# Latent attention: weighted values of two heads, block by block in turn, at the end of each pair of heads

## The chip, the cores and the metric

One NeuronCore of a Trainium2 chip runs the kernel. The metric is the device time of one execution in microseconds. PE is the matrix engine (TensorE), PEld its weight loads, DVE VectorE, ACT ScalarE, POOL GpSimd, SP the engine that issues most DMAs.

## The reference, cut to what matters

One layer of a decoder: half a feed-forward step, a mixer of two attention branches, another half feed-forward step, for 512 tokens of width 1024. The part that the change touches is the latent attention of the mixer, with 8 heads, query and key of 96 numbers, values of 64, causal over 512 tokens:

```python
def causal_dense_attention(q, k, v, scale):
    ...
    def one_block(args):
        qb, qp = args
        logits = jnp.einsum('bqhd,bkhd->bhqk', qb, k).astype(jnp.float32) * scale
        logits = jnp.where(k_pos[None, :] <= qp[:, None], logits, NEG_INF)
        p = jax.nn.softmax(logits, axis=-1)
        return jnp.einsum('bhqk,bkhd->bqhd', p.astype(v.dtype), v)
```

The last line is the product of probabilities and values. Its result goes on, with that of a dilated attention of 24 heads, through two projections, gates and an output projection.

## The kernel before, in words

All activations lie transposed, features on the partitions and the 512 tokens along the free axis. The program is one stream of weight pieces of 128 x 1024 numbers. Each is loaded by a DMA into `raw`, rounded by ScalarE into `w_hi` (`split_hi`, line 352), its rest taken by VectorE into `w_lo` (`split_lo`, line 357), and used by TensorE in three products per 128 x 128 tile (`multiply`, lines 370 to 372). The order of each engine's work is written out by hand, and engines wait for one another by semaphores; each engine runs its own list in order.

The latent stage does one head per turn, two heads per round of the loop (line 644), then heads 6 and 7 outside it. In head h TensorE does, in `attention` (line 616):

- `score` (line 567): the scores of head h into banks 2, 3 and 4, four blocks of 128 queries against all keys up to them, each with one product that adds the causal mask;
- `turn_values` (line 558): values of head h turned into bank 5, from where ScalarE copies them to `mla_v` (`take_values`, line 941);
- `lora` (line 548): key, value and query of head h + 1, 15 products; VectorE takes them in `take_lora` (lines 1295 to 1313), key and values (`mla_k`, `mla_vt`) first;
- `project` (line 517): 24 products of a gate, and ahead of the last two tiles of it, in `turn_early`, the probabilities of head h turned for the first key block (part 0) and the second (part 1). Head 7 has the first dilated projection in place of the gate, and no `lora`;
- `turn_probs(h, i, 2)`: the third and fourth key blocks turned (part 2);
- `attend` (line 599), once for each part: products of values and turned probabilities into bank 7. Key block k reaches queries from k on, so the four products are 512, 384, 256 and 128 columns wide. An even head fills partitions 0 to 63 of the bank, an odd one 64 to 127.

Parts go through banks 6, 5 and 6 and are copied by ScalarE (`take_probs`, line 953) to one of two buffers of `probs_t` in turn, so the third copy has to wait until the first part has been used (`pv_done`, line 960). Behind the three copies ScalarE has the gate's tanh (line 936) and the split of the next weights (line 352). VectorE has, per head, `maxima` (line 1316) on the scores, `take_lora` with `normalize` (line 1325) inside it, the splits of weights, and after an odd head `take_mixed` (line 1334), the copy of the pair's results out of bank 7. The lines that the rows below name are 961 (copies of turned probabilities), 610 (products with values), 595 (transposes), 579 and 581 (scores, mask), 1320 (maxima), 1308 (the next query is ready), 1313 (`mla_vt`).

The dilated stage behind it handles two heads at once, and its `attend_dil` (line 694) alternates between the two, head e in partitions 64 e to 64 e + 63 of bank 2 (lines 703 and 707).

Of the kernel before, what the change touches and what calls it, by code (L numbers as in the profile page):

```python
# [32 lines left out]
P = 128  # L33
SEQ = 512
BLOCKS = SEQ // P
# [11 lines left out]
PAIRS = GROUP_HEADS // 2  # L47
# [148 lines left out]
def decoder_layer(nc, x_t, positions, rel_bias, gains_in, tables, onehot_in, mask_in, ffn, w_latent, w_lora_up,  # L196
# [22 lines left out]
    with ctx:  # L219
# [44 lines left out]

        mixed = shared("mixed", [P, 2 * PAIRS, SEQ])
        gates = shared("gates", [P, 2 * KM, SEQ])
        probs_t = shared("probs_t", [P, 2, SEQ])
        lat_hi = shared("lat_hi", [P, KQ + KKV, SEQ], F32R)
        lat_lo = shared("lat_lo", [P, KQ + KKV, SEQ], F32R)
        sumsq_kv = shared("sumsq_kv", [P, SEQ])  # L270
# [4 lines left out]
        mla_q = shared("mla_q", [P, 2, SEQ])  # L275
        mla_k = shared("mla_k", [P, 2, SEQ])
        mla_vt = shared("mla_vt", [P, SEQ])
        mla_v = shared("mla_v", [P, BLOCKS, V_DIM])
        mla_p = shared("mla_p", [P, 10 * P])
        mask_ident = shared("mask_ident", [P, P], F32R)  # L280
        mask_causal = shared("mask_causal", [P, P], F32R)
# [182 lines left out]
        def _(pe):  # L464
# [102 lines left out]
            def score(h, i):  # L567

                pe.wait_ge(head_ready, h + 2 * i + 1)
                for b, (out, diagonal) in enumerate(((bank[2][:, 0:P], bank[2][:, 0:P]),
                                                     (bank[3][:, 0:2 * P], bank[3][:, P:2 * P]),
                                                     (bank[2][:, P:SEQ], bank[2][:, 3 * P:SEQ]),
                                                     (bank[4][:, :], bank[4][:, 3 * P:SEQ]))):
                    nc.tensor.matmul(out, mla_q[0:QK_DIM, h % 2, b * P:(b + 1) * P],  # L579
                                     mla_k[0:QK_DIM, h % 2, 0:(b + 1) * P], start=True, stop=False, skip_group_check=True)  # L580
                    last = nc.tensor.matmul(diagonal, mask_ident[:, :], mask_causal[:, :], start=False, stop=True,
                                            skip_group_check=True)
                last.then_inc(mla_scores, 1)
# [12 lines left out]
                        at += P  # L596
                last.then_inc(turned, 1)

            def attend(h, i, part):

                unit = 4 * h + 1 + part
                pe.wait_ge(turned_taken, unit + 8 * i + 1)
                row = V_DIM * (h % 2)
                at = 0
                for key in ((0,), (1,), (2, 3))[part]:
                    width = SEQ - key * P
                    last = nc.tensor.matmul(bank[7][row:row + V_DIM, key * P:SEQ], mla_v[:, key, :],  # L610
                                            probs_t[:, (3 * h + part) % 2, at:at + width],
                                            start=key == 0, stop=key == 3, skip_group_check=True)
                    at += width
                last.then_inc(pv_done, 1)

            def attention(h, i, s, d):

                score(h, i)
                turn_values(h, i)

                def turn_early(k):
                    if k == 6:
                        turn_probs(h, i, 0)
                        turn_probs(h, i, 1)

                if h < MLA_HEADS - 1:
                    lora(s, d, h + 1, i)
                    c = gate_chunk(h)
                    project(s + 1, d, c + 6 * i, bank[c % 2][:, :], turn_early)
                else:  # L630

                    c = CHUNKS["dil"]
                    project(PIECES["dil"], 0, c, bank[c % 2][:, :], turn_early)
                turn_probs(h, i, 2)
                for part in range(3):
                    attend(h, i, part)

            s = PIECES["mla"]

# [170 lines left out]
        def _(act):  # L810
# [127 lines left out]

            def take_values(h, i):
                act.wait_ge(turned, 4 * h + 8 * i + 1)  # L940
                nc.scalar.copy(mla_v[:, :, :].rearrange("p b n -> p (b n)"),
                               bank[5 + (4 * h) % 2][:, 0:BLOCKS * V_DIM]).then_inc(turned_taken, 1)

            def exponentials(h, i):
# [6 lines left out]
                                         accum_out=mla_stats[:, 2, b:b + 1]).then_inc(mla_exp, 1)  # L951

            def take_probs(h, i):
                for part, width in enumerate((4 * P, 3 * P, 3 * P)):
                    unit = 4 * h + 1 + part
                    act.wait_ge(turned, unit + 8 * i + 1)
                    n = 3 * h + part
                    if n >= 2:

                        act.wait_ge(pv_done, n + 6 * i - 1)  # L960
                    nc.scalar.copy(probs_t[:, n % 2, 0:width], bank[5 + unit % 2][:, 0:width]).then_inc(turned_taken, 1)

            def attention(h, i, s, d, following):

# [35 lines left out]
            def take_dil_probs(unit, i):  # L1000
                width = 3 * P if unit // 2 == 1 else SEQ
                act.wait_ge(turned, 4 * MLA_HEADS + unit + 8 * i + 1)

                act.wait_ge(pv_done, 3 * MLA_HEADS + unit + 8 * i - 1)
                nc.scalar.copy(probs_t[:, unit % 2, 0:width], bank[5 + unit % 2][:, 0:width]).then_inc(turned_taken, 1)

            def dilated_pair(i, first=False):
# [53 lines left out]
        def _(dve):  # L1061
# [288 lines left out]
            def attention(h, i, s, d, following):  # L1350


                maxima(h, i)
                if h < MLA_HEADS - 1:
                    take_lora(s, d, h + 1, i, lambda: normalize(h, i))
                    split_lo(dve, s + 2, d, following[0])
                    gate_take(s + d + 2, gate_chunk(h) % 2, h + 1 + 2 * i)
                    if following[1]:
                        split_lo(dve, s + 3, d, following[1])
                else:  # L1360
                    normalize(h, i)
                    split_lo(dve, s + 2, d, following[0])
                if h % 2:
                    take_mixed(h // 2 + i, 3 * h + 3 + 6 * i, bank[7][:, :])

            s = PIECES["mla"]
            take_lora(s, 0, 0, 0, query_norm_and_rotary_key)
# [105 lines left out]
            def dilated_pair(i, first=False):  # L1473
                s, d, c, e = PIECES["dil"], 12 * i, CHUNKS["dil"], 11 * i
                for q in range(12):
                    tiles = HALF if q in (9, 10) else TILES
                    if q or not first:
                        split_lo(dve, s + q + 1, d, tiles)
                    if q in (3, 5, 7):
                        dil_maxima(q // 2 - 1, i)  # L1480
                    if q < 6:
                        out = (dil_q, dil_k)[q % 2][:, q // 2, :]
                    else:
                        out = dil_vt[:, q % 2, :]
                    if q == 0 and not first:

                        take_mixed(PAIRS - 1 + i, 3 * MLA_HEADS + 8 * i, bank[2][:, :])
                    if q < 9:
                        take_projection(out, s + q, d, (c + q) % 2)
                    if q == 9:  # L1490
                        group_weights(i)
                        scale_probs(0)
                        gate_take(s + d + 10, (c + 9) % 2, MLA_HEADS + 2 * i)
                        for g in (1, 2):
                            scale_probs(g)
# [6 lines left out]

            for k in range(2 * PAIRS):
                if k == PAIRS:
                    take_mixed(2 * PAIRS - 1, 3 * MLA_HEADS + 8 * PAIRS, bank[2][:, :])
                dve.wait_ge(mixed_rounded, k + 1)
                nc.vector.tensor_tensor(act_lo[:, k, :], mixed[:, k, :], act_hi[:, k, :].bitcast(F32),
                                        ALU.subtract).then_inc(mixed_split, 1)
# [113 lines left out]
```

## Time and profile before

| | us |
|---|---|
| median of 3 runs | 1325.17 (1324.86 to 1326.73) |
| the profiled execution | 1325.78 |
| its span, first to last instruction | 1323.2 |
| TensorE busy | 1296.1 (98%) |
| VectorE busy | 673.4 (51%) |
| ScalarE busy | 437.9 (33%) |
| latent stage, heads 0 to 7, in the span | about 424 to 550 |

A matmul record in the profile has a start and a modelled end, and records of one engine overlap, so the distance from start to start tells what a product costs. An f32 product has two records and two weight loads. A line of the timeline that ends in x8 is eight records that lie together, from the first start to the last end.

### The profile page before, as it was taken

To read this page: it belongs to the slowest core of one execution; us is meant where nothing else is said; L and a number is where in the kernel's file an instruction comes from. 1 tells how busy PE (TensorE), PEld (TensorE's weight loads), DVE (VectorE), ACT (ScalarE), POOL (GpSimd) and SP (SyncE) were. 2 spreads that over 40 slices of the span, in tenths; PEclk is the share of its full clock that TensorE was granted. 3 is DMA by queue.
4 is the path that set the end of the run, shared out by engine and by line. 5 is a ranking of instruction groups with operands and counts; after the bars stand their busy time and mean duration, and the time that the engine had idled before them with its cause. 6 is when DMAs were issued, how large, how long until landed. Compare 5 with 4: busy or idle time off the path is not lost.

```text
span 1323.2 us, 16875 instructions
## 1 busy us (share of the span) xinstructions
PE 1296.1 (98%) x5984; PEld 1042.1 (79%) x5984; DVE 673.4 (51%) x947; ACT 437.9 (33%) x763; POOL 16.4 (1%) x34
## 2 busy tenths in 40 slices
PE   8999999999998999999999999999999999999996
PEld 5788888888886677788887878778888888888884
DVE  6744444433358666454554445476654444443324
ACT  5322223322243344243433333433432222332221
POOL 0000000000000000300000000000000000000000
PEclk9999999999999999999999999999999999999998
DMA  6243332233322211612222122223323322223321
GB/s 222 80 111 98 100 100 96 88 103 90 102 89 62 68 52 64 127 64 80 72 72 80 63 79 69 74 80 98 109 80 97 99 101 98 96 89 91 98 87 63
DMA packets 35920, 118.84 MB, mean 90 GB/s; under 512 B 4664, under 2 KB 4664, under 8 KB 35888
## 3 DMA queue, kind: packets, MB, share of 16 engines
q1 hardware_dynamic: 34272, 114.83, 27.1%
q0 software_dynamic: 1328, 3.56, 1.6%
q8 instruction: 19, 0.31, 0.1%
q14 instruction: 13, 0.11, 0.0%
q10 hardware_dynamic: 288, 0.03, 0.0%
HBM read 115.85 MB, written 2.55 MB: 89 GB/s over the span
## 4 chain that ended last, share of the span: by engine, by line
PE 90%; DVE 6%; ACT 2%; issue 1%; DMA 1%; SPq 0%; DVEq 0%; ACTq 0%
PE bank L370 27%; PE bank L372 27%; PE bank L371 27%; PE bank L667 2%; PE bank L610 1%; PE bank L579 1%; PE bank L690 1%; DVE w_lo L357 1%; ACT w_hi L352 1%; DVE rstd L1098 1%; DMA raw<-in_ffn_up 1%; PE bank L595 1%; PE bank L707 1%; PE bank L703 1%; PE bank L676 0%
## 5 line engine op out<-in xcount | busy, mean ns | idle before, releaser
L370 PE MATMUL bank<-act_hi,w_hi 128*128 128x512 f32 x1232 | 487.8, 396 | 7.7 <-DVE w_lo L357 3.6
L372 PE MATMUL bank<-act_hi,w_lo 128*128 128x512 f32 x1232 | 480.1, 390 | 0.0
L371 PE MATMUL bank<-act_lo,w_hi 128*128 128x512 f32 x1232 | 479.8, 389 | 0.0
L357 DVE TENSOR_TENSOR w_lo<-raw,w_hi 128x1024 fp32r<-128x1024 f32 (+3 forms) x222 | 260.3, 1172 | 240.3 <-ACT w_hi L352 236.1
L352 ACT ACTIVATE w_hi<-raw 128x1024 fp32r<-128x1024 f32 (+3 forms) x222 | 224.0, 1009 | 200.1 <-PE bank L372 199.7
L370 PEld LDWEIGHTS bank<-act_hi,w_hi 128*128 128x128 f32 x1232 | 231.3, 188 | 65.3 <-issue 8.9
L372 PEld LDWEIGHTS bank<-act_hi,w_lo 128*128 128x128 f32 x1232 | 231.3, 188 | 49.1
L371 PEld LDWEIGHTS bank<-act_lo,w_hi 128*128 128x128 f32 x1232 | 231.5, 188 | 46.7 <-issue 1.0
L372 PE MATMUL bank<-hid_hi,w_lo 128*128 128x512 f32 x352 | 136.9, 389 | 0.0
L370 PE MATMUL bank<-hid_hi,w_hi 128*128 128x512 f32 x352 | 136.9, 389 | 0.0
L371 PE MATMUL bank<-hid_lo,w_hi 128*128 128x512 f32 x352 | 136.9, 389 | 0.0
L859 ACT ACTIVATE hid_hi<-work 128x512 f32 (+1 forms) x44 | 27.8, 633 | 171.9 <-DVE work L1170 171.9
L857 ACT ACTIVATE work<-work 128x512 f32<-128x512 f32 x44 | 27.8, 632 | 154.9 <-DVE work L1164 154.9
L371 PEld LDWEIGHTS bank<-hid_lo,w_hi 128*128 128x128 f32 x352 | 66.1, 188 | 13.8
L370 PEld LDWEIGHTS bank<-hid_hi,w_hi 128*128 128x128 f32 x352 | 66.1, 188 | 13.7
L372 PEld LDWEIGHTS bank<-hid_hi,w_lo 128*128 128x128 f32 x352 | 66.1, 188 | 13.5
L1164 DVE TENSOR_TENSOR work<-bank,rstd 128x512 f32<-128x512 f32 x44 | 30.4, 691 | 63.0 <-PE bank L372 62.9
L1170 DVE TENSOR_TENSOR work<-bank,work 128x512 f32<-128x512 f32 x44 | 30.4, 692 | 56.0 <-PE bank L372 55.6
L1175 DVE TENSOR_TENSOR hid_lo<-work,hid_hi 128x512 f32 (+1 forms) x44 | 30.5, 693 | 43.1 <-ACT hid_hi L859 43.1
L993 ACT ACTIVATE dil_p<-dil_p,stats 128x128 f32<-128x128 f32 (+1 forms) x96 | 39.9, 416 | 37.0 <-DVE stats L1411 37.0
L817 ACT ACTIVATE act_hi<-x,gains 128x512 fp32r<-128x512 f32 (+1 forms) x24 | 16.9, 721 | 67.5 <-DVE x L1193 38.0
L1193 DVE SCALAR_TENSOR_TENSOR x<-bank,x 128x512 f32 (+1 forms) x16 | 11.1, 692 | 44.6 <-PE bank L372 44.6
(153 smaller groups left out, 929.2 us busy)
## 6 DMA issues: line engine op xcount, KB each, us to landing
raw<-in_ffn_gate SPq DMA_DIRECT2D x44, 512.0 KB, 3.4
raw<-in_ffn_up SPq DMA_DIRECT2D x44, 512.0 KB, 3.4
raw<-in_w_dil SPq DMA_DIRECT2D x40, 512.0 KB, 3.4
raw<-in_ffn_down SPq DMA_DIRECT2D x32, 448.0 KB, 3.3
raw<-in_ffn_down SPq DMA_DIRECT2D x16, 512.0 KB, 3.5
raw<-in_w_mla_gates SPq DMA_DIRECT2D x8, 512.0 KB, 3.4
raw<-in_w_branches SPq DMA_DIRECT2D x8, 512.0 KB, 3.4
raw<-in_w_out SPq DMA_DIRECT2D x8, 512.0 KB, 3.4
```

What stands on the lines that cost most here:

```text
L352: nc.scalar.activation(w_hi[:, s % SPLIT, 0:tiles * P], raw[:, s % RAW, 0:tiles * P], ACT.Copy).then_inc(hi_ready, 1)
L357: nc.vector.tensor_tensor(w_lo[:, s % SPLIT, 0:tiles * P], raw[:, s % RAW, 0:tiles * P], w_hi[:, s % SPLIT, 0:tiles * P].bitcast(F32), ALU ...
L370: nc.tensor.matmul(out, a, hi(k), start=first, stop=False)
L371: nc.tensor.matmul(out, a, lo(k), start=False, stop=False)
L372: last = nc.tensor.matmul(out, b, hi(k), start=False, stop=end)
L667: last = nc.tensor.matmul(out, dil_q[rows, g, tokens(g, b)], dil_k[rows, g, keys], start=True, stop=True, skip_group_check=True)
L857: nc.scalar.activation(work[:, 1, :], work[:, 0, :], ACT.Silu).then_inc(silu_ready, 1)
L859: nc.scalar.activation(hid_hi[:, bass.ds(2 * i + j, 1), :], work[:, 3:4, :], ACT.Copy).then_inc(hid_rounded, 1)
L993: nc.scalar.activation(p, p, ACT.Exp, bias=stats[:, 0, g, order, at:at + 1], accum_out=stats[:, 1, g, order, at:at + 1]).then_inc(dil_exp, 1)
L1164: nc.vector.tensor_tensor(work[:, 0, :], bank[c % UP_BANKS][:, :], rstd[:, :], ALU.mult).then_inc(chunk_taken, 1)
L1170: nc.vector.tensor_tensor(work[:, 3, :], bank[c % UP_BANKS][:, :], work[:, 2, :], ALU.mult).then_inc(chunk_taken, 1)
L1175: nc.vector.tensor_tensor(hid_lo[:, chunk, :], work[:, 3:4, :], hid_hi[:, chunk, :].bitcast(F32), ALU.subtract).then_inc(hid_split, 1)
```

## The change

The tile `probs_t` becomes 2 x 1280 numbers per partition instead of 2 x 512: all ten turned blocks of one head in each half, odd heads in one, even in the other. `mla_v` has two buffers, one per head of a pair. ScalarE's copies no longer wait for `pv_done`. `attend` runs after odd heads alone and does both heads: for each key block the product of the even head, then that of the odd head. `pv_done` goes up once per pair and no longer once per part, and the waits on it are counted anew (the copies of the dilated stage, `take_mixed`). Ahead of an odd head's scores TensorE waits for the even head's first two copies, a wait that `attend` of the even head had made before.

```diff
-        probs_t = shared("probs_t", [P, 2, SEQ])
+        probs_t = shared("probs_t", [P, 2, 10 * P])
...
-        mla_v = shared("mla_v", [P, BLOCKS, V_DIM])
+        mla_v = shared("mla_v", [P, 2, BLOCKS, V_DIM])
...
+                if h % 2:
+                    pe.wait_ge(turned_taken, 4 * h + 8 * i - 1)
                 pe.wait_ge(head_ready, h + 2 * i + 1)
...
-            def attend(h, i, part):
-
-
-
-
-                unit = 4 * h + 1 + part
-                pe.wait_ge(turned_taken, unit + 8 * i + 1)
-                row = V_DIM * (h % 2)
-                at = 0
-                for key in ((0,), (1,), (2, 3))[part]:
+            def attend(h, i):
+
+                for key in range(BLOCKS):
+                    part, at = ((0, 0), (1, 4 * P), (2, 7 * P), (2, 9 * P))[key]
+                    pe.wait_ge(turned_taken, 4 * h + 2 + part + 8 * i)
                     width = SEQ - key * P
-                    last = nc.tensor.matmul(bank[7][row:row + V_DIM, key * P:SEQ], mla_v[:, key, :],
-                                            probs_t[:, (3 * h + part) % 2, at:at + width],
-                                            start=key == 0, stop=key == 3, skip_group_check=True)
-                    at += width
+                    for e in range(2):
+                        last = nc.tensor.matmul(bank[7][V_DIM * e:V_DIM * (e + 1), key * P:SEQ], mla_v[:, e, key, :],
+                                                probs_t[:, e, at:at + width], start=key == 0, stop=key == BLOCKS - 1,
+                                                skip_group_check=True)
                 last.then_inc(pv_done, 1)
...
                 turn_probs(h, i, 2)
-                for part in range(3):
-                    attend(h, i, part)
+                if h % 2:
+                    attend(h, i)
...
-                nc.scalar.copy(mla_v[:, :, :].rearrange("p b n -> p (b n)"),
+                nc.scalar.copy(mla_v[:, h % 2, :, :].rearrange("p b n -> p (b n)"),
...
-                for part, width in enumerate((4 * P, 3 * P, 3 * P)):
+                for part, (at, width) in enumerate(((0, 4 * P), (4 * P, 3 * P), (7 * P, 3 * P))):
                     unit = 4 * h + 1 + part
                     act.wait_ge(turned, unit + 8 * i + 1)
-                    n = 3 * h + part
-                    if n >= 2:
-
-                        act.wait_ge(pv_done, n + 6 * i - 1)
-                    nc.scalar.copy(probs_t[:, n % 2, 0:width], bank[5 + unit % 2][:, 0:width]).then_inc(turned_taken, 1)
+                    nc.scalar.copy(probs_t[:, h % 2, at:at + width], bank[5 + unit % 2][:, 0:width]).then_inc(turned_taken, 1)
...
-                    take_mixed(h // 2 + i, 3 * h + 3 + 6 * i, bank[7][:, :])
+                    take_mixed(h // 2 + i, h // 2 + i + 1, bank[7][:, :])
```

The end of an even head on TensorE, before (`const,mla_p` are the transposes of probabilities, `probs_t,mla_v` the products with values, `mla_k,mla_q` the next head's scores):

```order
L595 MATMUL bank<-const,mla_p 128x128 [waits turned_taken]
L595 MATMUL bank<-const,mla_p 128x128 x2
L610 MATMUL bank<-probs_t,mla_v 64x512 [waits turned_taken]
L605 REGISTER_ALU
L610 MATMUL bank<-probs_t,mla_v 64x384 [waits turned_taken]
L610 MATMUL bank<-probs_t,mla_v 64x256 [waits turned_taken]
L610 MATMUL bank<-probs_t,mla_v 64x128
L574 REGISTER_ALU
L579 MATMUL bank<-mla_k,mla_q 128x128 [waits head_ready]
L581 MATMUL bank<-mask_causal,mask_ident 128x128
```

The same place in the changed program:

```order
L597 MATMUL bank<-const,mla_p 128x128 [waits turned_taken]
L597 MATMUL bank<-const,mla_p 128x128 x2
L575 REGISTER_ALU
L576 REGISTER_ALU [waits turned_taken]
L581 MATMUL bank<-mla_k,mla_q 128x128 [waits head_ready]
L583 MATMUL bank<-mask_causal,mask_ident 128x128
```

The four products are gone from here, and the scores follow the transposes.

The end of an odd head on TensorE, in the changed program:

```order
L597 MATMUL bank<-const,mla_p 128x128 [waits turned_taken]
L597 MATMUL bank<-const,mla_p 128x128 x2
L608 MATMUL bank<-probs_t,mla_v 64x512 [waits turned_taken]
L608 MATMUL bank<-probs_t,mla_v 64x512
L605 REGISTER_ALU
L608 MATMUL bank<-probs_t,mla_v 64x384 [waits turned_taken]
L608 MATMUL bank<-probs_t,mla_v 64x384
L608 MATMUL bank<-probs_t,mla_v 64x256 [waits turned_taken]
L608 MATMUL bank<-probs_t,mla_v 64x256
L608 MATMUL bank<-probs_t,mla_v 64x128 [waits turned_taken]
L608 MATMUL bank<-probs_t,mla_v 64x128
```

Each width stands twice, even head first, and the waits are for ScalarE's copies of the odd head.

## Rows read from the trace of the kernel before

**Rows 1.** The page: busy time of each engine, and the chain that ended last.

```profile
PE 1296.1 (98%) x5984; PEld 1042.1 (79%) x5984; DVE 673.4 (51%) x947; ACT 437.9 (33%) x763; POOL 16.4 (1%) x34
...
PE 90%; DVE 6%; ACT 2%; issue 1%; DMA 1%; SPq 0%; DVEq 0%; ACTq 0%
```

**Rows 2.** Busy time by stretches: stretch, length, PE, PEld, DVE, ACT, POOL, PE clock, DMA.

```profile
430.00:560.00 130.00, 128.13 (x590) 92.81 (x589) 80.44 (x150) 49.44 (x118) 12.71 (x24) 1.00 0.29 75
```

**Rows 3.** The same view, line 610 alone: PE and PEld busy, clock, DMA.

```profile
439.62:442.06 2.44, 2.44 (x8) 0.93 (x8) 1.00 0.47 134
...
547.82:550.31 2.49, 2.49 (x8) 0.93 (x8) 1.00 0.49 194
sum 19.59, PE 19.58 PEld 7.42; mean PE 2.45 PEld 0.93
```

**Rows 4.** Timeline of TensorE, end of head 0: start, duration, work.

```profile
439.20 0.49 PE L595 MATMUL bank<-const,mla_p 128*128 128x128 f32 x3
439.62 2.50 PE L610 MATMUL bank<-probs_t,mla_v 128*64 128x512 f32 x8
442.06 0.49 PE L579 MATMUL bank<-mla_k,mla_q 96*128 96x128 f32 x2
```

**Rows 5.** The same, windows 439.65 to 440.05, then to 440.20.

```profile
439.42 0.27 PE L595 MATMUL bank<-const,mla_p 128*128 128x128 f32 x1
439.62 0.64 PE L610 MATMUL bank<-probs_t,mla_v 128*64 128x512 f32 x1
...
439.62 1.07 PE L610 MATMUL bank<-probs_t,mla_v 128*64 128x512 f32 x2
```

**Rows 6.** The same, dilated stage, windows to 612.10, to 612.30, to 612.95.

```profile
611.90 0.44 PE L703 MATMUL bank<-probs_t,dil_v 128*64 128x256 f32 x2
...
611.90 0.65 PE L703 MATMUL bank<-probs_t,dil_v 128*64 128x256 f32 x4
...
611.90 1.08 PE L703 MATMUL bank<-probs_t,dil_v 128*64 128x256 f32 x8
612.91 0.33 PE L690 MATMUL bank<-const,dil_p 128*128 128x128 f32 x1
```

**Rows 7.** Busy time by stretches, instructions on `dil_v` alone: PE, clock, DMA.

```profile
618.66:619.68 1.02, 1.02 (x16) 1.00 0.00 0
```

**Rows 8.** Waits of the weight loader, heads 0 to 7: total us, times, longest.

```profile
PEld bank L610 <- ACT probs_t L961: 4.8, 8, 0.6
```

**Rows 9.** Timeline of ScalarE, head 0 (in brackets: idle before, and what ended it).

```profile
437.69 0.97 ACT L961 COPY probs_t<-bank 128x512 f32<-128x512 f32 x2 [3.49 <-PE bank L595]
440.73 0.48 ACT L961 COPY probs_t<-bank 128x384 f32<-128x384 f32 x1 [2.07 <-PE bank L610]
...
441.73 1.05 ACT L352 ACTIVATE w_hi<-raw 128x1024 fp32r<-128x1024 f32 x1
```

**Rows 10.** Timeline of VectorE, end of head 0 and start of head 1.

```profile
437.25 0.68 DVE L1308 TENSOR_TENSOR mla_q<-mla_q,rotated 32x512 f32<-32x512 f32 x1
...
442.81 1.23 DVE L357 TENSOR_TENSOR w_lo<-raw,w_hi 128x1024 fp32r<-128x1024 f32 x1 [2.72 <-ACT w_hi L352]
444.92 1.69 DVE L1320 TENSOR_REDUCE mla_stats<-bank 128x1 f32<-128x128 f32 x4 [0.89 <-PE bank L581]
```

**Rows 11.** Timelines of VectorE and TensorE: head 0's maxima, then both gate projections.

```profile
429.51 1.68 DVE L1320 TENSOR_REDUCE mla_stats<-bank 128x1 f32<-128x128 f32 x4
...
432.01 0.69 DVE L1313 TENSOR_TENSOR mla_vt<-bank,rstd_kv 64x512 f32<-64x512 f32 x1
...
432.84 0.49 PE L370 MATMUL bank<-act_hi,w_hi 128*128 128x512 f32 x1 [0.87 <-DVE mla_vt L1313]
...
448.73 0.39 PE L370 MATMUL bank<-act_hi,w_hi 128*128 128x512 f32 x1
```

**Rows 12.** Weight loads: line 610's (ns min/median/max), then the timeline in the dilated stage.

```profile
L610 PEld LDWEIGHTS bank<-probs_t,mla_v x64: 132/136/137, 439.6 to 550.0; 128*64 128x64 f32 x64
...
611.89 0.63 PEld L703 LDWEIGHTS bank<-probs_t,dil_v 128*64 128x64 f32 x8 [0.36 <-ACT probs_t L1005]
```

More of the change, by code:

```diff
@@ L1002, in take_dil_probs @@
                 act.wait_ge(turned, 4 * MLA_HEADS + unit + 8 * i + 1)
-                act.wait_ge(pv_done, 3 * MLA_HEADS + unit + 8 * i - 1)
+                act.wait_ge(pv_done, PAIRS + unit + 8 * i - 1)
                 nc.scalar.copy(probs_t[:, unit % 2, 0:width], bank[5 + unit % 2][:, 0:width]).then_inc(turned_taken, 1)
@@ L1485, in dilated_pair @@
                     if q == 0 and not first:
-                        take_mixed(PAIRS - 1 + i, 3 * MLA_HEADS + 8 * i, bank[2][:, :])
+                        take_mixed(PAIRS - 1 + i, PAIRS + 8 * i, bank[2][:, :])
                     if q < 9:
@@ L1504, in _ @@
                 if k == PAIRS:
-                    take_mixed(2 * PAIRS - 1, 3 * MLA_HEADS + 8 * PAIRS, bank[2][:, :])
+                    take_mixed(2 * PAIRS - 1, PAIRS + 8 * PAIRS, bank[2][:, :])
                 dve.wait_ge(mixed_rounded, k + 1)
```

## Prediction

> **What bounds the kernel now.** I read the page first: TensorE is busy for 98% of the span, VectorE for 51%, ScalarE for 33%, and the chain that ended last is 90% TensorE work [rows 1]. So a microsecond taken out of TensorE's queue is a microsecond of the whole, as long as the other engines keep up. The table by stretches says that this holds where the change is, in the latent stage, and that the clock granted there is full: 128.13 of 130 us busy at 1.00 [rows 2]. At full clock (the 2.4 GHz level) nothing is to be won or lost from the clock, and I take none.
>
> Then I cut out the weighted values alone. Each head spends 2.44 us on them from the first record of `bank<-probs_t,mla_v` to the first record of what follows, the last two heads 2.49; eight stretches make 19.59 us, 1.5% of the span [rows 3]. In head 0 they lie between the last transposes and the next head's scores with nothing of another kind in between [rows 4]. That is the whole of what the change can speed up directly.
>
> How do those 2.44 us arise? Each of the four products of a head is an f32 product and leaves two records. A window of TensorE's timeline that ends at 440.05 holds one 512-column record, one that ends at 440.20 holds two, and together they last 1.07 against 0.64 us: the second starts 0.43 us behind the first [rows 5]. So the records of one head run in turn, 512 columns per 0.43 us. For 512 + 384 + 256 + 128 = 1,280 columns in two records each this makes 2 x 1,280 x 0.43 / 512 = 2.15 us, and 0.29 us are left for the way in, the way out and a stall. Each such product fills 64 of the array's 128 columns (128*64 in the rows).
>
> The trace already has the pattern that the change brings, in the dilated stage: there the two heads of a pair alternate product by product, one head's result in partitions 0 to 63 of the bank, the other's in 64 to 127. Two 256-column records start together at 611.90 and take 0.44 us in all, four take 0.65 (in turn the second alone would end there), and from the first of eight to the start of the next kind of work at 612.91 it is 1.01 us [rows 6]. In turn the eight would take 8 x 0.43 / 2 = 1.72 us. In pairs they take 4 x 0.215 = 0.86, and 0.15 is left for way in and out. The sixteen 128-column records say the same: 1.02 us [rows 7] against 16 x 0.107 = 1.72 in turn and 0.86 in pairs.
>
> **The change, part by part.**
>
> *Even heads (0, 2, 4, 6)* lose their whole stretch: TensorE goes from the third group of transposes straight to the next head's scores. That removes 3 x 2.44 + 2.49 = 9.81 us.
>
> *Odd heads* now do both heads, 16 records, alternating. If they pair up as in the dilated stage, the time is 2 x (0.43 + 0.32 + 0.215 + 0.107) = 2.14 us, plus the 0.15 of way in and out from [rows 6]: 2.29 us, where 2.44 or 2.49 stood. Four stretches of 2.29 are 9.2 us; against 19.6 that is **10.4 us less**.
>
> *The stall inside a head.* Before, the third copy of turned probabilities waited until the first product had freed its buffer, and the weight loads of the third product waited for that copy: 4.8 us in all over eight heads, 0.6 at most [rows 8]. Most of it is not lost on TensorE, since a product was still running; what is lost is part of the 0.29 us above. With both heads' probabilities kept, the copy doesn't wait for a product, and it overlaps the first four products of the pair (1.5 us against a copy of 0.48). It is already counted: the 2.29 has no stall. Nothing is late next there.
>
> *The new wait ahead of an odd head's scores* (the first two copies of the even head must be done). In head 0 these copies end at 437.69 + 0.97 = 438.66 [rows 9], and the scores would want to start at 439.62, where the products stood [rows 4]. It costs nothing, with 0.96 us to spare. Behind it stand the scores and all else of the next head, so a late ScalarE would be felt at once. The scores also want the query of the next head, which VectorE has ready at 437.25 + 0.68 = 437.93 [rows 10]: 1.7 us to spare.
>
> *ScalarE after an even head.* The third copy now starts when its transposes are done (439.20 + 0.49 [rows 4], about 439.8) and not at 440.73. The gate's tanh and the split of the next weights are queued behind it and move with it, by 0.95 us; in the rows of before the split starts at 441.73 [rows 9], so it starts near 440.8 and VectorE's half of the split, which stood at 442.81 [rows 10], near 441.9.
>
> *VectorE after an even head.* Here the cover is thin. The scores now end 2.44 us sooner, so the maxima could start at 444.92 - 2.44 = 442.48, but the split of weights stands ahead of them on VectorE and ends at 441.9 + 1.23 = 443.1. The maxima are 0.6 us late against TensorE. From their start to the end of `mla_vt` it takes 432.01 + 0.69 - 429.51 = 3.19 us when nothing is waited for, so `mla_vt` is done at 446.3, and TensorE starts 0.14 us behind it (432.70 and 432.84 in head 0, where the same lateness costs 0.87 us once [rows 11]). The gate projection would want to start at 448.73 - 2.44 = 446.29 [rows 11]. So it stands for about 0.1 us in each of heads 0, 2 and 4; after head 6 no such products follow. I put **0.3 us** on this. Bounds: nothing, if ScalarE's part moves up by 0.1 more; and if nothing of ScalarE's moved up, the split would end at 444.04 and the stall would be 1.0 us, 3 us over three heads.
>
> *Odd heads, other engines.* ScalarE's third copy and what is behind it move up by the same 0.95 us while TensorE's products shrink by 0.15 only. The copy of the finished pair out of the bank stands between the split and the maxima as before, and has more room. Buffers: the larger tiles cost memory and no instruction. The loads of weights are released by the split, and TensorE waits for none of them here.
>
> *Switches of the array's mode.* Between the last transpose and the first product, and again before the scores, the weight loader pauses; of eight such pairs four go. The stretches of [rows 3] run from start to start, so this is inside the 2.44 already.
>
> The sum: 10.4 - 0.3 = 10.1 us less. The profiled execution took 1325.78 us (span 1323.2 and 2.6 around it), so 1315.7 for it; the median of the runs shown is 0.6 lower, and my number is **1315.1 us**.
>
> **A rule against it.** The rows show eight loads of 64 columns done within 0.63 us while the paired products of the dilated stage run [rows 12]; a load alone takes 0.137. The Trainium skill ("TensorE: Matmul & The Clock Gate", Part 3, on packing small matmuls) says that a weight load overlaps running products only when its row group differs. Here both heads use all 128 rows and differ in columns only. By that rule the 16 loads of a pair would stand bare.
>
> **The rivals.**
>
> *Loads or products don't overlap between the two heads.* With 16 bare loads of 0.137 us, the pair takes 2.29 + 2.19 = 4.5 us; with products in turn 2 x 2.36 - 0.15 = 4.57. Either way 0.3 to 0.4 us per pair is won against 4.88, in all about 1.5 us: **1323.6 us**, no change to be told. [Rows 6, 12] speak against it. For it speaks only that the trace of before has no 512-column products that alternate. Chance 0.04.
>
> *Only half pairing.* If a head's second record has to wait behind its first while the other head's has not begun, the 16 records take one 512-column step more: 2.29 + 0.43 = 2.72 us per pair, and the gain is 8.4 us: 1316.8. Chance 0.12.
>
> *VectorE becomes the bound after even heads.* With 1.0 us of stall in three heads, as bounded above, the gain is 7.4 us: 1317.8. The row of 0.87 us in [rows 11] shows that the mechanism is real; the copy that moves up speaks against its full size. Chance 0.13.
>
> *Slower: alternating costs a switch each time.* The Trainium skill ("TensorEngine Tiling (Array Packing)", Key Properties) says that a change of tiling mode drains the engine, and that a change of tile alone doesn't. If on this chip the step from one half of the columns to the other did, there would be 15 such steps in 16 records or 7 between the products. By rows: products in turn, 4.57 us, and 7 steps of 0.20 us, the largest distance that the transposes show ahead of a change (439.42 to 439.62 [rows 4, 5]), make 5.97 against 4.88, 4.4 us more in all: **1329.6 us**. It is slower from 0.05 us a step. The two records that start together in [rows 6] exclude it, unless 512 columns differ from 256. Chance 0.02.
>
> **How the numbers follow.** Forecast 0.69, half pairing 0.12, VectorE 0.13, no overlap 0.04, switches 0.02. A measurement of this kernel tells about 0.2%, 2.6 us, from no change. The first three are all faster by more than that, so faster 0.94; no change 0.04; slower 0.02. The likely case alone spans 1314.3 (no stall, and a better way out of even heads by 0.1 each) to 1316.4. The range reaches to the half pairing and to VectorE's bound with some room for the chip: 1313.4 to 1318.2.
>
> **What would show it.** In the profile after: the products in four stretches of about 2.3 us, each with 16 records, two 512-column records starting together; no product between an even head's transposes and the next scores; a full clock. For the small term: TensorE idle before the gate projection put down to `mla_vt`, 0.1 us in three heads. Stretches of 4.5 us would make me wrong on the pairing, idle of about 1 us behind even heads wrong on VectorE, and a gain in the latent stage that the span doesn't show would mean that the dilated stage waits for something else than TensorE.

## The result, and the profile after

The changed kernel takes 1318.97 us (median of 4 executions, 1318.42 to 1319.48), the kernel before, run beside it, 1325.93 (4 executions, 1324.86 to 1326.73). The medians lie 7.0 us apart, a ratio of 0.9948; the ratio on record, which is not taken from these two medians alone, is 0.9941, 95% interval 0.9928 to 0.9953 (6.2 to 9.5 us). Either way the kernel is faster, clear of the noise. The profiled execution took 1319.48 us against 1325.78, its span 1317.5 against 1323.2.

The forecast was 1315.1 us, a gain of 10.1, with a range of 1313.4 to 1318.2: the direction is right, the time lies 0.8 us above the range, and 3 of the 10 us are missing. The kernel before was 0.8 us slower in this comparison than the 1325.17 that the forecast starts from; as a gain the range was 7.0 to 11.8 us, and the measured gain lies at its lower edge. Where the missing 3 us are is the subject of this part. The page first, busy time and the chain that ended last, against [rows 1]:

```profile
PE 1291.8 (98%) x5984; PEld 1043.4 (79%) x5984; DVE 672.7 (51%) x947; ACT 438.5 (33%) x763; POOL 16.4 (1%) x34
...
PE 89%; DVE 6%; ACT 2%; issue 1%; DMA 1%; DVEq 0%; SPq 0%; ACTq 0%
```

Nothing has changed sides: TensorE is 98% busy. The products with values, in the busy time by stretches (PE, PEld, clock, DMA), against [rows 3]:

```profile
457.23:459.53 2.30, 2.30 (x16) 1.05 (x16) 1.00 0.53 142
486.46:488.75 2.29, 2.29 (x16) 1.06 (x16) 1.00 0.54 143
515.69:517.98 2.29, 2.29 (x16) 1.06 (x16) 1.00 0.78 222
542.26:544.56 2.30, 2.30 (x16) 1.06 (x16) 1.00 0.58 217
sum 9.18, PE 9.18 PEld 4.23; mean PE 2.29 PEld 1.06
```

Four stretches of 16 records in 9.18 us stand where eight of 8 records took 19.59. The timeline of TensorE shows the pair, in windows that end at 457.60 and at 457.80, against [rows 5]:

```profile
457.23 0.65 PE L608 MATMUL bank<-probs_t,mla_v 128*64 128x512 f32 x2
...
457.23 1.08 PE L608 MATMUL bank<-probs_t,mla_v 128*64 128x512 f32 x4
```

Two 512-column records last 0.65 us where one lasted 0.64, and four last 1.08 where two lasted 1.07. The two heads run at the same time. At the end of head 0 the scores follow the transposes directly, against [rows 4]:

```profile
443.21 0.49 PE L597 MATMUL bank<-const,mla_p 128*128 128x128 f32 x3
443.54 0.28 PE L581 MATMUL bank<-mla_k,mla_q 96*128 96x128 f32 x1
```

So 10.4 us of products are gone, and the span is only 5.7 shorter. Two things took most of the rest. The first is in the busy time by stretches of TensorE alone (PE busy, clock, DMA), before the first changed instruction has run:

```profile
422.00:425.00 3.00, 1.26 (x6) 1.00 0.00 0
425.00:426.00 1.00, 0.49 (x3) 0.83 0.00 0
426.00:435.00 9.00, 9.00 (x24) 0.50 0.31 96
435.00:436.00 1.00, 1.00 (x4) 0.55 0.00 0
436.00:445.00 9.00, 9.00 (x48) 1.00 0.14 38
```

TensorE had stood still ahead of head 0's scores (2.25 us by the wait on the row below), and then its clock was at the lower of its two levels, 1.2 GHz, for some 10 us: 24 records in nine of them. The same stretches of the kernel before:

```profile
422.00:425.00 3.00, 0.86 (x4) 1.00 0.00 0
425.00:426.00 1.00, 0.90 (x6) 1.00 0.00 0
426.00:435.00 9.00, 8.13 (x36) 1.00 0.30 96
```

There the idle time is the same and the clock stayed full. The first score after the wait, in the changed kernel, then in the kernel before:

```profile
425.51 0.68 PE L581 MATMUL bank<-mla_k,mla_q 96*128 96x128 f32 x2 [2.25 <-DVE mla_q L1301]
```

```profile
425.10 0.49 PE L579 MATMUL bank<-mla_k,mla_q 96*128 96x128 f32 x2 [2.24 <-DVE mla_q L1308]
```

From these scores to the first transposes of head 0 it takes 15.6 us (425.51 to 441.07) in the changed kernel and 11.9 (425.10 to 437.05) before. That is 3.6 us for the lower clock, and it hides the 0.87 us of [rows 11], which is idle time no longer. The scores themselves start 0.4 us later than before (425.51 against 425.10), ahead of any instruction that differs, so 0.4 us of the two spans' difference is the start of the execution.

The second thing is what the prediction had as a small term. In the timeline of the changed kernel, last product of `lora` and first of the gate behind it, after head 0:

```profile
449.89 0.39 PE L372 MATMUL bank<-lat_hi,w_lo 128*128 128x512 f32 x1
450.45 0.49 PE L370 MATMUL bank<-act_hi,w_hi 128*128 128x512 f32 x1 [0.17 <-DVE mla_vt L1306]
```

From start to start 0.56 us, where without a wait it is 0.23 (448.51 to 448.73 before). The same place after heads 2 and 4 has 0.52 and 0.51. So TensorE loses 0.33 + 0.29 + 0.28 = 0.9 us. And the product behind such a wait holds up the next one by 0.1:

```profile
450.78 0.39 PE L371 MATMUL bank<-act_lo,w_hi 128*128 128x512 f32 x1
```

which is 0.33 us behind its forerunner and not 0.23. Together the three waits cost 1.2 us, where 0.3 was forecast. The column "idle" shows only 0.17 of the first, since it counts from the modelled end of the last product: the distance of starts is what tells.

### The profile page after: what moved, and what is told of

It reads as the page before. It is cut to its first block, busy times and chain, and to the rows that moved or that the text cites. A ratio compares the mean times of both kernels' runs of the same rounds, so it can differ in the third digit from the quotient of the medians.

```text
span 1317.5 us, 16858 instructions
## 1 busy us (share of the span) xinstructions
PE 1291.8 (98%) x5984; PEld 1043.4 (79%) x5984; DVE 672.7 (51%) x947; ACT 438.5 (33%) x763; POOL 16.4 (1%) x34
## 4 chain that ended last, share of the span: by engine, by line
PE 89%; DVE 6%; ACT 2%; issue 1%; DMA 1%; DVEq 0%; SPq 0%; ACTq 0%
PE bank L370 28%; PE bank L372 27%; PE bank L371 27%; PE bank L664 2%; PE bank L581 1%; PE bank L687 1%; DVE w_lo L357 1%; ACT w_hi L352 1%; DVE rstd L1091 1%; PE bank L608 1%; DMA x<-in_x_t 1%; PE bank L597 1%; PE bank L704 1%; PE bank L700 1%; DVE mla_stats L1313 1%
```

## The experiments

**First the clock.** Both kernels again, unchanged, in more executions, and both with the idle time ahead of head 0's scores filled. The filled kernels have, at the end of TensorE's work ahead of the loop, products of constants into a bank that is free there; nobody reads their results:

```diff
             project(s + 1, 0, gate_chunk(-1), bank[gate_chunk(-1) % 2][:, :])
+            for width in (SEQ, SEQ, 2 * P):
+                nc.tensor.matmul(bank[6][:, 0:width], ident, const[:, C_EXPAND:C_EXPAND + width], start=True, stop=True)
```

The kernel before, again:

> The kernel before, unchanged, to see in several executions whether the clock granted to TensorE stays full through the idle time ahead of head 0's scores. Theory A (the lower clock of the changed kernel from 425.8 to 435.5 us is a matter of where the idle time of 2.9 us happens to fall, not of the new order, which begins later): some executions here show a mean clock near 0.992 and are about 3 us longer than the others. Theory B (the change causes it): all executions show 0.997 and lie within 1 us of 1325.5.

Measured: 12 executions from 1324.39 to 1329.98, median 1327.76, mean clocks from 0.991 to 0.997. The times go with the clock: three at 0.997 (1324.39 to 1325.64), three at 0.994 (1326.65 to 1326.80), six at 0.991 and 0.992 (1328.73 to 1329.98).

The changed kernel, again:

> The changed kernel, unchanged, again in several executions. Theory A: some executions show a mean clock of 0.997 and about 1316 us, the others 0.992 and 1319. Theory B: all show 0.992 and 1319.

Measured: two executions at 0.997 (1314.97 and 1315.04), two at 0.994 (1316.79, 1316.80), two at 0.992 (1319.11, 1319.23). Theory A holds in both kernels: the lower clock comes in the kernel before just as well, in 9 of these 12 executions. At like clocks the changed kernel is faster by 9.9 to 10.3 us: 1325.25, the middle of the three at 0.997, against 1315.0; 1326.7 against 1316.8; 1329.3, the median of the six, against 1319.2. In the first comparison all four executions of the changed kernel had 0.992 or 0.993, while the one clock that is recorded for the kernel before is 0.997; by their times two of its four executions (1324.86, 1325.17) belong to the full clock and two (1326.69, 1326.73) to the middle group. The middle group has a shorter stretch at the lower level; the profile of such an execution of the changed kernel shows it (TensorE alone, as above):

```profile
422.00:426.00 4.00, 1.76 (x10) 1.00 0.00 0
426.00:427.00 1.00, 1.00 (x4) 0.61 0.65 118
427.00:433.00 6.00, 6.00 (x17) 0.50 0.37 124
433.00:434.00 1.00, 1.00 (x6) 0.98 0.00 0
```

Of the kernel before no execution with a lower clock was profiled: that its slow stretch lies in the same place is argued from its mean clocks and from the next run.

The kernel before with the idle time filled:

> The kernel before with three products of constants into a free bank (512, 512 and 256 columns, 2.1 us) in TensorE's idle time ahead of head 0's scores. Both theories: the clock stays full there. It should measure as the kernel before does at full clock, 1325.2, or up to 0.3 us more if the last of them delays the scores.

Measured: 1324.94 (11 executions, 1324.14 to 1325.22), clocks 0.995 to 0.997. Adding work makes this kernel faster than the unfilled one beside it (ratio 0.9981, interval 0.9971 to 0.9991), and its times lie within 1.1 us and not 5.6.

The changed kernel, filled:

> The changed kernel with the same three products. If the lower clock is what hid the rest of the gain, the clock is full and the time is about 1316.0 (9.4 us below the filled kernel before: 10.5 of products less 1.0 of stalls behind VectorE). If something else keeps the gain down to 7 us, it stays near 1319.

Measured: **1314.74** (5 executions, 1314.34 to 1315.04), all at 0.996 or 0.997, ratio to the unfilled kernel before 0.9909 (0.9895 to 0.9922). Against the filled kernel before it is 10.2 us faster. TensorE in its timeline, the filling products and the scores behind them:

```profile
422.13 2.31 PE L642 MATMUL bank<-const 128*128 128x512 f32 x6
424.52 0.49 PE L581 MATMUL bank<-mla_k,mla_q 96*128 96x128 f32 x2
```

and no 2.2 us of idle time. The scores start 0.6 us earlier than those of the filled kernel before (425.15), and nothing differs between the two programs up to there, so 0.6 of the 10.4 us between the two profiled spans is the start of the execution and not the change.

**Then the gain, part by part**, all with the filling products. The runs of this part and of the next come from a second chip, the last two runs from a third. The fastest executions of the unfilled kernel before were 1324.42, 1324.38 and 1324.91 us on the three, so a few tenths between medians of different chips tell nothing, and lengths within one profile are given beside them.

The two heads in series at the end of a pair:

```diff
-                for key in range(BLOCKS):
-                    part, at = ((0, 0), (1, 4 * P), (2, 7 * P), (2, 9 * P))[key]
-                    pe.wait_ge(turned_taken, 4 * h + 2 + part + 8 * i)
-                    width = SEQ - key * P
-                    for e in range(2):
+                for e in range(2):
+                    for key in range(BLOCKS):
+                        part, at = ((0, 0), (1, 4 * P), (2, 7 * P), (2, 9 * P))[key]
+                        pe.wait_ge(turned_taken, 4 * (h - 1 + e) + 2 + part + 8 * i)
+                        width = SEQ - key * P
```

> The changed kernel with the three filling products, but at the end of a pair the four products of the even head come first and then the four of the odd head; nothing else differs. Theory A (the gain comes from products of the two heads that run at the same time in different columns): the stretch goes from 2.30 to about 4.57 us per pair, and the time is 9.1 us above the filled changed kernel, near 1323.8. Theory B (the gain comes from the waits and the fewer changes between kinds of work, and alternating adds little): the stretch stays near 2.3 to 3, and the time within 2 us of 1314.7.

Measured: 1321.10 (1320.64 to 1321.59), 6.4 us above the alternating one. Theory A is right in kind and 2.7 us off in size. The stretch is 3.86 us and not 4.57, as the timeline of TensorE and the chain of the same stretch show:

```profile
452.89 3.93 PE L608 MATMUL bank<-probs_t,mla_v 128*64 128x512 f32 x16
456.75 0.49 PE L581 MATMUL bank<-mla_k,mla_q 96*128 96x128 f32 x2
```

```profile
452.96 2.30 PE bank L608 x8
455.36 1.46 PE bank L608 x6
```

Four such stretches are 4 x (3.86 - 2.30) = 6.2 us longer, which is what was measured. A window of the timeline that begins at 454.62 shows why they aren't longer still:

```profile
454.44 0.65 PE L608 MATMUL bank<-probs_t,mla_v 128*64 128x256 f32 x2
```

Two records lie there from 454.44, 0.65 us together. A 256-column record of the even head would be over after 0.38 (the odd head's last one stands alone at 456.22 and lasts that long), so the other is the odd head's first 512-column record: it started when the even head's 256 columns did, although a second record of those and two of the 128 columns are written ahead of it and had not begun. The seam of the two heads overlaps by itself. It doesn't overlap earlier. A window from 454.45 to 454.60 has three records:

```profile
454.12 0.97 PE L608 MATMUL bank<-probs_t,mla_v 128*64 128x384 f32 x3
```

They are the even head's last 384-column record, which started at 454.12, and the two of 454.44. At 454.12 four records stood ahead of the odd head's first, and that one did not start, although its columns were free and ScalarE had copied its probabilities by 451.93.

Each head on its own, with both heads' probabilities kept, so that no copy waits for a product:

```diff
-                    for e in range(2):
+                    for e in (h % 2,):
...
-                last.then_inc(pv_done, 1)
+                if h % 2:
+                    last.then_inc(pv_done, 1)
...
-                if h % 2:
-                    attend(h, i)
+                attend(h, i)
```

> Both heads' probabilities and values are kept as in the changed kernel and no copy waits for a product, but each head does its own four products at its own end, as before; filled. Theory A: only the stall of about 0.08 us inside each head goes, 8 x 0.08 = 0.6 us, so 1324.3 against 1324.9 of the filled kernel before. Theory B (the waits carry the gain): several us below 1324.9.

Measured: 1323.69 (10 executions, 1323.06 to 1323.95), 1.25 us below the filled kernel before; 0.6 was expected. The eight stretches in its timeline are 2.29 us each, as the first of them:

```profile
439.93 2.37 PE L608 MATMUL bank<-probs_t,mla_v 128*64 128x512 f32 x8
442.22 0.38 PE L581 MATMUL bank<-mla_k,mla_q 96*128 96x128 f32 x1
```

The stall that the wait for the buffer makes is thus 0.15 us per head (2.44 less 2.29), and not the 0.08 that I had read from the starts of single records. With this the gain of 10.2 us has its parts: 1.2 from the waits, 2.6 more when both heads stand at the end of the pair in series (1323.69 to 1321.10), 6.4 from alternating. In the profiles the latent stage, from head 0's first score to the first product behind the last ones with values, is 125.2, 123.8, 121.6 and 115.5 us long in the filled kernel before and these three: steps of 1.4, 2.2 and 6.1. The middle step is no effect of the waits: the overlap at the seam and the way in and out that the pair pays once make a stretch 0.7 us shorter than two of 2.29, 2.9 us in all; the even heads' shorter way to the next scores gives nearly 0.8 more, and the stall behind VectorE, which appears here too (0.56, 0.55 and 0.55 us from start to start), takes about 1.3 back. So most of the gain, in series and alternating together, is products of the two heads running at the same time.

**Then the stall behind VectorE.** ScalarE rounds the gate's weights before the gate's tanh:

```diff
                 take_probs(h, i)
+                if following[1]:
+                    split_hi(act, s + 3, d, following[1])
                 if h < MLA_HEADS - 1:
                     gate_tanh(gate_chunk(h) + 6 * i, h + 1 + 2 * i)
-                if following[1]:
-                    split_hi(act, s + 3, d, following[1])
```

> The changed kernel, filled, with ScalarE's rounding of the gate's weights ahead of the gate's tanh instead of behind it. If the idle time of TensorE ahead of the gate projections of heads 1, 3 and 5 (about 0.3 us each) comes from VectorE's split of those weights standing late ahead of the maxima, it goes, and the time falls by 1.0 us from 1314.7 to 1313.7. If it comes from the maxima and the rest of VectorE's list, the time stays at 1314.7.

Measured: 1313.65 (1313.23 to 1313.90), 1.1 us less, as expected; the latent stage of the profile is 1.3 us shorter (115.5 to 114.2). VectorE after head 0, first in the filled changed kernel:

```profile
441.39 1.22 DVE L357 TENSOR_TENSOR w_lo<-raw,w_hi 128x1024 fp32r<-128x1024 f32 x1 [1.87 <-ACT w_hi L352]
442.54 1.68 DVE L1315 TENSOR_REDUCE mla_stats<-bank 128x1 f32<-128x128 f32 x4
```

then with the exchange:

```profile
440.42 1.23 DVE L357 TENSOR_TENSOR w_lo<-raw,w_hi 128x1024 fp32r<-128x1024 f32 x1 [1.10 <-ACT w_hi L352]
441.56 1.68 DVE L1315 TENSOR_REDUCE mla_stats<-bank 128x1 f32<-128x128 f32 x4
```

The split ends 0.96 us sooner and the maxima start 0.98 us sooner, of which 0.2 is the earlier start of this execution (its copy of the probabilities is 0.21 earlier). In TensorE's timeline the last product of `lora` and the gate's first, without and with the exchange, go from 0.56 apart to 0.23:

```profile
445.31 0.39 PE L372 MATMUL bank<-lat_hi,w_lo 128*128 128x512 f32 x1
445.87 0.49 PE L370 MATMUL bank<-act_hi,w_hi 128*128 128x512 f32 x1 [0.17 <-DVE mla_vt L1308]
```

```profile
445.14 0.39 PE L372 MATMUL bank<-lat_hi,w_lo 128*128 128x512 f32 x1
445.37 0.39 PE L370 MATMUL bank<-act_hi,w_hi 128*128 128x512 f32 x1
```

The same exchange in the filled kernel before, as a control:

> The same exchange on ScalarE in the filled kernel before, as a control. There TensorE has no such idle time behind even heads except ahead of head 1's projections of the first round, which the exchange doesn't touch: 1324.9, unchanged, within 0.3 us.

Measured: 1324.61 (1324.24 to 1325.43), 0.3 us below 1324.94, within the spread of both and on another chip: no gain can be told. Behind heads 0 to 6 the exchange is worth something only where the change has made VectorE late.

**How close must the alternation be?** On top of the filled changed kernel with the exchange on ScalarE, two products of each head at a time:

```diff
-                for key in range(BLOCKS):
+                for e, key in ((0, 0), (0, 1), (1, 0), (1, 1), (0, 2), (0, 3), (1, 2), (1, 3)):
```

> On top of the filled kernel with ScalarE's rounding first (1313.65): at the end of a pair the even head's 512 and 384 columns, then the odd head's, then the even head's 256 and 128, then the odd head's. In the run with the heads in series the odd head's first product started while three records of the even head, written ahead of it, had not started. Theory A (a product can start ahead of up to three earlier records that wait for the other columns): the first products of both heads start together here too, the stretch stays at 2.3 to 2.5 us, and the time at 1313.7 to 1314.5. Theory B (only neighbours in the order pair up): the stretch grows to at least 3.2 us, and the time to 1317 or more.

Measured: 1313.98 (1313.60 to 1314.91) against 1313.65. The timeline of TensorE, in a window that ends at 453.60 and in a longer one:

```profile
453.42 0.66 PE L608 MATMUL bank<-probs_t,mla_v 128*64 128x512 f32 x2
...
453.42 2.42 PE L608 MATMUL bank<-probs_t,mla_v 128*64 128x512 f32 x16
455.77 0.49 PE L581 MATMUL bank<-mla_k,mla_q 96*128 96x128 f32 x2
```

Both heads start together, with three records of the even head (the second of 512 columns, two of 384) written in between, and the stretch is 2.35 us. Theory A holds: a product for the free columns goes ahead of three earlier records that wait for the other columns. The 0.3 us between the medians is as expected from four stretches longer by 0.05, and too small to be told between two chips.

**The best version.** The same exchange ahead of the loop, for head 0:

```diff
-            gate_tanh(gate_chunk(-1), 0)
             split_hi(act, s + 3, 0, TILES)
+            gate_tanh(gate_chunk(-1), 0)
```

> The filled kernel with ScalarE's rounding first, and the same exchange once more ahead of the loop, so that VectorE's split of the first gate's weights doesn't stand late ahead of head 0's maxima. If the idle time of 0.9 to 1.1 us ahead of the gate projection in head 0 has the same cause as that behind the even heads, it goes: 1312.6. If not, 1313.6.

Measured: **1312.05** (4 executions, 1311.96 to 1312.21), ratio to the kernel before 0.9883 (0.9865 to 0.9902), which makes it the fastest of all. It is 1.6 us below the kernel without this exchange, where 1.0 was expected; the wait in head 0 cost 1.1 us by the distance of starts (430.96 to 432.26 against 0.23) and 0.1 behind it. The latent stages of the two profiles differ by just this, 1.2 us (114.2 to 113.0); the other 0.4 lies between two chips and stays unexplained. Of TensorE's waits in the latent stage one is left, at head 7, which no edit here touches:

```profile
PE bank L597 <- DVE mla_p L1327: 0.9, 1, 0.9
```

## Why the prediction was right or wrong

*The pairing*, the step with 2.29 us per pair: right to 0.01 us (2.30, 2.29, 2.29, 2.30), and with it the 10.4 us of products. That 512 columns pair up as 256 did was carried over from [rows 6, 7], and held. Sixteen loads of 0.137 us, 2.2 us in all, stand within a stretch of 2.30 that is as long as one head's with eight loads, so they overlap running products of the same rows. The rule of the Trainium skill ("TensorE: Matmul & The Clock Gate", Part 3) that spoke against it, overlap only where the row group differs, does not hold here (the same part also lets a load overlap that goes to a background weight buffer; no run here tells whether these did), and the trace of before could have told: one head's eight loads make 1.1 us, its products in turn 2.15, and the stretch is 2.44 [rows 3, 12]. Half pairing, products in series and a switch at each step are excluded by the same rows.

*The whole, at full clock*: 10.1 us forecast; 9.9 to 10.3 measured at like clocks, 10.2 in the filled kernels. Term by term, products: -10.4 forecast, -10.4 measured. The way from an even head's transposes to the next head's products: 0 to 0.1 us less was forecast; the scores now start 0.33 us behind the first transpose where 0.42 of that way was left before (442.06 - 439.20 - 2.44), and they are 0.1 shorter up to the first product of `lora` (3.04 us, 443.54 to 446.58, against 3.14, 442.06 to 445.20), so nearly 0.2 for each of four heads. The stall behind VectorE: +0.3 forecast, +1.2 measured. The sum is -9.9. In the two filled profiles the latent stage, counted as before, is 9.7 us shorter (425.15 to 550.33, and 424.52 to 540.03). Two errors of the small terms, opposite in sign, nearly cancel in the total; the agreement of the total is better than its parts.

*The stall behind VectorE* was mis-sized by four. The mechanism was named rightly, and the exchange on ScalarE shows it. VectorE's own chain was right: 3.20 us from the maxima to the end of `mla_vt` (442.54 to 445.74), 3.19 forecast. What failed is the line "The gate projection would want to start at 448.73 - 2.44 = 446.29": counted from the first of the last transposes, TensorE is there after 6.91 us (438.63 to 445.54) and not 7.09, for the two reasons just given. The maxima came within 0.02 us of where they were put (3.91 us behind that transpose, 438.63 to 442.54), and with the 0.14 us from `mla_vt` to TensorE the prediction's own numbers made 0.14 per head, which it rounded to 0.1. So 0.14 and 0.18 make the 0.33 us of head 0. The 0.1 behind each wait was not counted at all. A slack that comes out as 0.1 us from several steps of 0.1 should have been given as 0 to 0.4 per head.

*The sentence on the clock* is the step that failed, and it cost the most: "nothing is to be won or lost from the clock, and I take none". It rested on one execution whose clock was full. [Rows 2] begin behind the idle time, and a look at 422 to 425 would have shown TensorE still for more than 2 us between two dense stretches. One execution can't show that such a place is a coin toss, but it can show that the place exists. In the comparison the toss fell unevenly and took 3 of the 10 us: 4.0 from the changed kernel (1318.97 against 1315.0), 0.7 from the kernel before (1325.93 against 1325.25). That the forecast of 10.1 us agrees with the gain at like clocks so closely is partly luck, as the terms above show. The price of the lower clock is in the three groups of either kernel: 1.5 to 2 us for the short stretch, about 4 us for the long one.

*The single stall inside a head* was put at part of 0.29 us, later at 0.08; it is 0.15. It was inside the 2.44 us and changed no sum of the prediction, only the expectation of one experiment.

*The new wait ahead of odd scores, the copies, the buffers and the dilated stage* cost nothing, as forecast: after the last products of the pair of heads 6 and 7, 772.9 us follow in both kernels (1317.5 - 544.56, and 1323.2 - 550.31).

## What to carry to other kernels

When two products use half of the array's columns each, place their results in different halves of the partitions and near one another in the order, here with at most three records between: they took the time of one. When TensorE's work shrinks, ask for each wait that it has behind it how many tenths of a microsecond are left, and which engine's list decides that; an exchange of two instructions on ScalarE gave back 1.1 of the 1.2 us that the change had lost there. And where TensorE stands still for 2 us or more between dense stretches, compare executions at like clocks, or fill the gap, before a difference of 0.3% is put down to an edit.

## What the runs showed that I had not expected

The order of the records doesn't have to alternate strictly: a product started up to three records ahead of its place when those waited for the other half of the columns (0.6 us overlapped at the seam of two heads in series, and the whole stretch at 2.35 us with two products at a time). In all four stretches of the run in series it started with three records left ahead of it and not with four, though its columns were free and its data copied; whether the limit lies in the number of records or in the weight loads between them was not tried. The same part of the Trainium skill says that matmuls start and end in strict order of the program; the odd head's 512-column record of 454.44 in the run with the heads in series started ahead of three earlier ones.

An unchanged kernel measured from 1324.4 to 1330.0 us on the same chip, and its times go with the mean clock; in the changed kernel, and by inference in this one, that is one stretch of lower clock after one idle time; 2.3 us of products that nobody needs cut the spread to 1.1 us. What decides whether the clock falls after this idle time, and for how long, was not found: it came and stayed away in executions of the same program.
